# GpSimd makes the rotation table and the C powers of the second to fourth state space batch; the fine table is laid by group

## Chip, cores and metric

One Trainium2 chip, one of its cores. The metric is the device time of one execution in microseconds, lower is better; the time of a kernel is the median of its runs.

## The reference

A trunk of two layers is applied to two requests (512 and 256 tokens of width 1024) with shared weights, in float32. Layer 0 mixes tokens with two head groups side by side, a state space mixer (S5) and a gated linear attention; layer 1 with differential attention. Each is followed by cross-attention and an MLP. The change lies in the S5 mixer of layer 0, which for 32 groups of 16 channels with 64 complex states computes, in both directions:

```python
lam_bar = jnp.exp(lam * step)
b_bar = ((lam_bar - 1.0) / lam)[..., None] * b
bu = jnp.einsum('gpc,blgc->blgp', b_bar, u)
# scan over l: s[l] = lam_bar * s[l-1] + bu[l]
return jnp.einsum('gcp,blgp->blgc', c, states).real
```

and then `gelu(y_fwd + y_bwd + d * u)`. Outputs are the trunk's results for both requests.

## The kernel before

`mixer_in` projects the input of layer 0 by 17 weight tiles of 128x1024 (numbers 0 to 16; each split into a rounded high part by ScalarE and a residue by DVE in `low`, L477) and computes S5 in between. All 768 tokens lie along the free axis, cut into 96 chunks of `SC` = 8 steps. The 32 groups go in `NB` = 4 batches of `GB` = 8 groups.

In a batch everything inside a chunk is matrix products, and the recurrence runs over the 96 chunks. Its steps:
- `dve_vv`: on DVE, B times powers of lam_bar for the batch, 12 instructions of 128x512; `pe_vt` transposes them.
- `dve_cl` (L497): on DVE, C times powers, the tile `cl`, two halves of 6 instructions of 128x640, each `cl<-cc,qf`, `tmp<-cc,qf`, `cl<-cl,tmp`. From the second batch on it waits for y_done, since TensorE reads the old `cl` until then.
- `pe_lag` (L368): products of `cl` and `bbar`, 64 short matmuls; waits for the semaphore m_cl. `act_rt` copies them out, `dve_rt` (L525) adds the diagonal and signals m_rtr.
- `pe_bu` (L379): the chunk inputs; waits for m_rtr and for the load of u.
- `dve_rot` (L514): on DVE, the rotation table `rot` (cosine and sine of the chunk's angle) from `fine` (16 small steps) and `coarse` (6 large ones), four multiplications of 128x768 with broadcast operands and two additions.
- `dve_main` (L531): turns the chunk inputs by `rot`, scans over the chunks, turns back, and signals m_st (below: S). `pe_y` (L388) then forms y and signals m_yd.
- `dve_gelu`, `act_tanh`, `dve_gelu_end`, `store_y`.

Each engine runs its own list in written order, and engines meet only by semaphores; `Chain` makes an engine wait for its own last result where the next instruction reads it. TensorE's order from S of one batch to `pe_bu` of the next is: `pe_y`, `pe_vt`, a weight tile (t3), `pe_lag`, a weight tile (t4, in the first transition alone), `pe_bu`; then tiles t1 and t2 beside `dve_main`:

```python
BATCH = [(6, 7, 8, 9), (10, 11, 12, 17), (13, 14, 15, 17), (16, 17, 17, 17)]
```

17 means no tile. On SP's DMA queue `load_u` of the next batch stands behind the store of a v tile, which waits until TensorE has transposed it, after its tile t3. GpSimd has no instruction in the mixer.

Of the kernel before, what the change touches and what calls it, by code (L numbers as in the profile page):

```python
# [123 lines left out]
def build(nc, params, x_in, mem_in, wt_in, wglu_in, wgate_in, bc_in, tab_in, u_dram, y_dram, k_dram, v_dram, qk_dram, vog_dram,  # L124
          lr_dram, out):
    ctx = ExitStack()
    with ctx:
        def sb(name, shape, dt=F32, on=ctx):
            return on.enter_context(nc.sbuf_tensor(name, shape, dt))
# [36 lines left out]
        def mixer_in():  # L166
# [13 lines left out]
            S = {n: sm[:, i, :] for i, n in enumerate(names)}  # L180
            fine = sb("s5fine", [P, 2, 17, G], on=fs)
            coarse = sb("s5coarse", [P, 2, 6, G], on=fs)
# [3 lines left out]
            qr = sb("qr", [P, 2, SC, G], on=fs)  # L186
            pw = sb("pw", [P, 2, SC + 1, G], on=fs)
            bin_ = sb("bin", [P, 2, G, GC], on=fs)
            dd = sb("dd", [GC, G, GC], on=fs)
# [32 lines left out]
            sqd, acd, ssum, sroot, an, ah, ar = (sig(f"m_{n}") for n in ("sqd", "acd", "ssum", "sroot", "an", "ah", "ar"))  # L222
            dec_ready = sig("m_dec")
            ud, ul, t_v, vt_done, vt_ready, cl_ready, lag_done, rt_copied, rt_ready, m_loaded = (sig(f"m_{n}") for n in (
# [265 lines left out]

            def dve_cl(v, b):
                spare = stf if b == 0 else free_words
                tmp = spare[:, 0:4 * POS * GC].rearrange("p (g n c) -> p g n c", g=4, n=POS)
                if b > 0:
                    v.wait_ge(y_done.sem, b)
                for h in range(2):
                    hs = slice(GB * b + 4 * h, GB * b + 4 * h + 4)  # L497
                    cb = [cc[:, i, hs, :].unsqueeze(2).to_broadcast([P, 4, POS, GC]) for i in range(2)]
                    qb = [qf[:, i, :, hs].rearrange("p n g -> p g n").unsqueeze(3).to_broadcast([P, 4, POS, GC]) for i in range(2)]
                    o = [cl[:, i, 4 * h:4 * h + 4] for i in range(2)]  # L500
                    for i, op in ((0, ALU.add), (1, ALU.subtract)):
                        nc.vector.tensor_tensor(o[i], cb[0], qb[i], ALU.mult)
                        dve_chain(nc.vector.tensor_tensor(tmp, cb[1], qb[1 - i], ALU.mult))
                        last = nc.vector.tensor_tensor(o[i], o[i], tmp, op)
                        if h == 1 and i == 1:
                            last.then_inc(cl_ready.sem, 1)
                        else:
                            dve_chain(last)

            def dve_rot(v, b):  # L510
                gs = slice(GB * b, GB * b + GB)
                four = [t_.rearrange("p (g a c) -> p g a c", g=GB, c=16) for t_ in (sq3[:, 0, :], sq3[:, 1, :])]
                o = [t_[:, :, :].rearrange("p g (a c) -> p g a c", c=16) for t_ in rot]
                f = [fine[:, i, 0:16, gs].rearrange("p c g -> p g c").unsqueeze(2).to_broadcast([P, GB, 6, 16]) for i in range(2)]  # L514
                c = [coarse[:, i, :, gs].rearrange("p a g -> p g a").unsqueeze(3).to_broadcast([P, GB, 6, 16]) for i in range(2)]
                nc.vector.tensor_tensor(o[0], f[0], c[0], ALU.mult)
                if b > 0:
                    v.wait_ge(yg_ready.sem, b)
                nc.vector.tensor_tensor(four[0], f[1], c[1], ALU.mult)
                nc.vector.tensor_tensor(o[1], f[0], c[1], ALU.mult)  # L520
                dve_chain(nc.vector.tensor_tensor(four[1], f[1], c[0], ALU.mult))
                nc.vector.tensor_tensor(o[0], o[0], four[0], ALU.subtract)
                dve_chain(nc.vector.tensor_tensor(o[1], o[1], four[1], ALU.add))

            def dve_rt(v, b):  # L525
# [5 lines left out]
            def dve_main(v, b, first, second):  # L531
                low(v, first)
                v.wait_ge(bu_done.sem, b + 1)
                bur = banks(4, 1024).rearrange("p (g j) -> p g j", j=P)[:, :, 0:NCH]
                bui = banks(6, 1024).rearrange("p (g j) -> p g j", j=P)[:, :, 0:NCH]
# [55 lines left out]
            with nc.Block() as block:  # L591
# [86 lines left out]
                def _(a):  # L678
# [69 lines left out]
                    act_chain.close()  # L748

                @block.vector  # L750
                def _(v):
# [72 lines left out]
                    v.wait_ge(t_v.sem, 1)  # L824
                    dve_cl(v, 0)
                    low(v, 4)
# [4 lines left out]
                    late = quarters(sq3[:, 1:3, :])  # L831
                    for to in (fine, coarse):
                        nc.vector.memset(to[:, 0, 0, :], 1.0)
                        nc.vector.memset(to[:, 1, 0, :], 0.0)
                    cmul(fine[:, 0, 1, :], fine[:, 1, 1, :], S["p4r"], S["p4i"], S["p4r"], S["p4i"], tmp)
                    for n in (1, 2, 4, 8):
                        powers(fine, n, n, n, late)
                    nc.vector.tensor_copy(coarse[:, 0, 1, :], fine[:, 0, 16, :])
                    dve_chain(nc.vector.tensor_copy(coarse[:, 1, 1, :], fine[:, 1, 16, :]))
                    powers(coarse, 1, 1, 1, late)  # L840
# [3 lines left out]
                                                      ident[0:GC, 0:GC].unsqueeze(1).to_broadcast([GC, G, GC]), ALU.mult))  # L844
                    dve_rot(v, 0)
                    nc.vector.tensor_scalar(gains[:, 1:2], pcol("dnorm"), 1.0 - LAMBDA_INIT, None, ALU.mult)
# [6 lines left out]
                    for b in range(NB):  # L853
                        t1, t2, t3_, t4_ = BATCH[b]
                        dve_main(v, b, t1, t2)
                        if b + 1 < NB:
                            low(v, t3_)
                            dve_vv(v, b + 1)
                        if b == NB - 1:
                            for k in range(4):  # L860
                                dve_mem_apply(v, k)
                            for k in range(4):
                                dve_mem_residue(v, k)
                                dve_mem_apply(v, k + 4)
                            dve_mem_residue(v, 4)
                            dve_mem_residue(v, 5)
                        dve_gelu(v, b)
                        if b + 1 < NB:
                            dve_cl(v, b + 1)
                        dve_gelu_end(v, b)  # L870
                        if b == NB - 1:
                            dve_mem_residue(v, 6)
                            dve_mem_residue(v, 7)
                        if b + 1 < NB:
                            low(v, t4_)
                            dve_rot(v, b + 1)
                            dve_rt(v, b + 1)
# [1514 lines left out]
```

## Time and profile before

| | |
|---|---|
| median of 3 runs | 2552.81 us (2550.39 to 2553.39) |
| profiled execution | 2552.52 us, its span 2550.7 us |
| TensorE busy | 2441.4 us, 96% |
| DVE busy | 1531.6 us, 60% |
| ScalarE busy | 1149.9 us, 45% |
| GpSimd busy | 0.2 us |

The mixer with its four batches takes the first 289 us of it; the state space batches lie between 91 and 284 us. The execution's own time is 1.8 us longer than the span, which is what lies outside the trace.

### The profile page before, as it was taken

The page shows a single profiled execution, that of the slowest core. Times are in us where ns is not written, and L with a number is a line of the kernel's source. Part 1 is how long each engine was busy: PE and PEld are TensorE (multiplying, and loading weights), DVE is VectorE, ACT ScalarE, POOL GpSimd, SP SyncE. Part 2 cuts the span into 40 slices and gives each one's busy share as a digit, 9 for nine tenths or more (in the row PEclk, how much of TensorE's full clock was granted, in tenths as well). Part 3 has the DMA queues.
Part 4 walks back from the last instruction along what each step waited for, and adds up shares of the span by engine and source line. Part 5 has one row for each costly group of instructions (what it writes and reads, how often), then busy time and mean ns, then how long its engine had stood idle before and what let it go on. Part 6 is the DMA issues. An engine that isn't in the chain of part 4 may idle for free.

```text
span 2550.7 us, 35203 instructions
## 1 busy us (share of the span) xinstructions
PE 2441.4 (96%) x14102; PEld 2073.6 (81%) x14102; DVE 1531.6 (60%) x2587; ACT 1149.9 (45%) x2003; POOL 0.2 (0%) x4
## 2 busy tenths in 40 slices
PE   7997699899998999999999999999999999999999
PEld 4887576778887999899778888778788888888887
DVE  8998766767546655565565446566886545633332
ACT  4332336445433555544454344445665443433322
POOL 0000000000000000000000000000000000000000
PEclk9998899999999999999999999999999999999999
DMA  5324432255321455444224323223324322433232
GB/s 189 94 75 96 154 117 90 83 170 191 110 75 58 149 183 183 131 125 137 86 75 149 116 79 120 75 83 104 94 92 135 115 91 91 141 99 94 96 99 91
DMA packets 109667, 289.24 MB, mean 113 GB/s; under 512 B 18913, under 2 KB 41569, under 8 KB 108225
## 3 DMA queue, kind: packets, MB, share of 16 engines
q1 hardware_dynamic: 101392, 261.36, 33.1%
q10 hardware_dynamic: 8112, 25.63, 3.0%
q8 instruction: 113, 1.85, 0.3%
q14 instruction: 50, 0.40, 0.0%
HBM read 265.35 MB, written 19.50 MB: 112 GB/s over the span
## 4 chain that ended last, share of the span: by engine, by line
PE 76%; DVE 8%; ACT 3%; issue 1%; ACTq 0%; DVEq 0%
PE ps L1381 65%; PE ps L1469 2%; PE ps L1444 2%; PE ps L1487 1%; DVE wlo L1358 1%; PE ps L1511 1%; DVE ps L1662 1%; DVE ps L1661 1%; DVE yP L1663 1%; ACT yP L1530 1%; PE ps L1413 1%; PE ps L1892 1%; DVE ringP L1733 1%; PE ps L1500 0%; ACT yP L1531 0%
## 5 line engine op out<-in xcount | busy, mean ns | idle before, releaser
L1381 PE MATMUL ps<-in_hP,whi 128*128 128x512 f32 x1344 | 544.9, 405 | 6.6 <-DVE wlo L1358 2.8
L1358 DVE TENSOR_TENSOR wlo<-wraw,whi 128x1024 fp32r<-128x1024 f32 x432 | 524.7, 1218 | 35.8 <-ACT whi L1353 35.6
L1353 ACT ACTIVATE whi<-wraw 128x1024 fp32r<-128x1024 f32 x432 | 454.2, 1052 | 188.0 <-PE ps L1381 129.5
L1381 PE MATMUL ps<-in_hP,wlo 128*128 128x512 f32 x1344 | 526.8, 392 | 0.0
L1381 PE MATMUL ps<-in_lP,whi 128*128 128x512 f32 x1344 | 525.9, 391 | 0.0
L1381 PE MATMUL ps<-in_hS,whi 128*128 128x256 f32 x1088 | 320.1, 294 | 7.4 <-DVE x L1684 4.3
L1381 PEld LDWEIGHTS ps<-in_hP,whi 128*128 128x128 f32 x1344 | 254.2, 189 | 69.3 <-issue 11.3
L1381 PE MATMUL ps<-in_lS,whi 128*128 128x256 f32 x1088 | 309.5, 284 | 0.0
L1381 PE MATMUL ps<-in_hS,wlo 128*128 128x256 f32 x1088 | 309.4, 284 | 0.0
L1684 DVE TENSOR_TENSOR x<-ps,x 128x256 f32<-128x256 f32 (+1 forms) x192 | 106.9, 557 | 331.6 <-PE ps L1381 331.2
L1381 PEld LDWEIGHTS ps<-in_lP,whi 128*128 128x128 f32 x1344 | 254.3, 189 | 56.0 <-issue 5.0
L1381 PEld LDWEIGHTS ps<-in_hP,wlo 128*128 128x128 f32 x1344 | 253.8, 189 | 54.7
L1381 PEld LDWEIGHTS ps<-in_hS,whi 128*128 128x128 f32 x1088 | 210.3, 193 | 23.0 <-issue 16.7
L1381 PEld LDWEIGHTS ps<-in_lS,whi 128*128 128x128 f32 x1088 | 210.5, 193 | 2.3 <-issue 1.4
L1381 PEld LDWEIGHTS ps<-in_hS,wlo 128*128 128x128 f32 x1088 | 210.3, 193 | 0.0
L1381 PE MATMUL ps<-hid_hP,whi 128*128 128x512 f32 x512 | 202.0, 395 | 0.0
L1381 PE MATMUL ps<-hid_hP,wlo 128*128 128x512 f32 x512 | 199.4, 389 | 0.0
L1381 PE MATMUL ps<-hid_lP,whi 128*128 128x512 f32 x512 | 199.4, 389 | 0.0
L1694 DVE TENSOR_TENSOR hid_lP<-ps,hid_hP 128x512 fp32r<-128x512 f32 x64 | 44.3, 692 | 231.9 <-ACT hid_hP L1586 231.9
L1584 ACT ACTIVATE ps<-ps 128x512 f32<-128x512 f32 (+1 forms) x128 | 60.8, 475 | 244.8 <-PE ps L1381 244.8
L1381 PE MATMUL ps<-hid_hS,whi 128*128 128x256 f32 x512 | 147.8, 289 | 1.9 <-DVE x L1684 1.9
L1381 PE MATMUL ps<-hid_lS,whi 128*128 128x256 f32 x512 | 144.8, 283 | 0.0
(464 smaller groups left out, 3659.1 us busy)
## 6 DMA issues: line engine op xcount, KB each, us to landing
wraw<-wt SPq DMA_DIRECT2D x432, 512.0 KB, 3.5
wraw<-wt ACTq DMA_DIRECT2D x17, 512.0 KB, 4.2
k_scratch<-region_P SPq DMA_DIRECT2D x16, 256.0 KB, 3.1
v_scratch<-vtmp SPq DMA_DIRECT2D x32, 128.0 KB, 3.1
x<-x_in SPq DMA_DIRECT2D x4, 768.0 KB, 7.0
mix_u<-x SPq DMA_DIRECT2D x32, 64.0 KB, 3.3
mix_mem<-mem_in ACTq DMA_DIRECT2D x4, 512.0 KB, 6.4
x<-x_in ACTq DMA_DIRECT2D x1, 2048.0 KB, 12.8
```

The source lines that it names most:

```text
L1353: nc.scalar.activation(whi[:, n % NHI, :, :], wraw[:, ws(n), :, :], ACT.Copy).then_inc(wh.sem, 1)
L1358: nc.vector.tensor_tensor(wlo[:, ws(n), :, :], wraw[:, ws(n), :, :], whi[:, n % NHI, :, :].bitcast(F32), ALU.subtract).then_inc(wr.sem, 1)
L1381: last = nc.tensor.matmul(ps[:, m % 2, 0:N[prod.g]], w_[:, k, :], x_[:, k, :], start=(k == 0 and j == 0), stop=(k == KT - 1 and j == 2))
L1413: nc.tensor.matmul(ps[:, 2, 0:s.n], s.mat, ring[g][:, i % 2, :], start=True, stop=True).then_inc(z["ssum"].sem, 1)
L1444: last = nc.tensor.matmul(ps[:, 3 + q_ % 2, b * 256:(b + 1) * 256], qx[g][:, 2 * h + j, lo:lo + P], km[g][:, 2 * h + j, :], start=(j == 0) ...
L1469: last = nc.tensor.matmul(ps[:, 7, j * 256:(j + 1) * 256], vm[g][:, kt, (2 * h + j) * P:(2 * h + j + 1) * P], at[:, q_ % 2, kt * 256:(kt + ...
L1487: last = nc.tensor.matmul(ps[:, 3 + zz, 0:N[g]], dq[g][rows, h, b * P:(b + 1) * P], dk[g][rows, h, :], start=True, stop=True)
L1511: last = nc.tensor.matmul(ps[:, 6 + h % 2, b * P:(b + 1) * P], dv[g][:, j, h * P:(h + 1) * P], at[:, q_ % 2, j * P:(j + 1) * P], start=(j ...
L1530: act_chain(nc.scalar.activation(s.to[:, 0:s.n], ps[:, s.bank, 0:s.n], ACT.Ln, bias=pcol("eps"), scale=1.0 / s.width))
L1584: act_chain(nc.scalar.activation(acc_ps, acc_ps, ACT.Relu))
L1684: nc.vector.tensor_tensor(x[:, i, cols(g)], ps[:, b, 0:N[g]], x[:, i, cols(g)], ALU.add).then_inc(tf[b].sem, 1)
L1694: nc.vector.tensor_tensor(hid_l[g][:, i, :], ps[:, b, 0:N[g]], hid_h[g][:, i, :].bitcast(F32), ALU.subtract)\
```

## The change

`dve_cl` and `dve_rot` stay on DVE for the first batch alone. For batches 1 to 3 a new GpSimd list holds `pool_rot` and `pool_cl` with the same instructions. `pool_rot` waits for m_st of the batch before, since DVE reads the old table until then; it puts its intermediate products into memory of tables no longer used (`turned`, in `s5tabs`), and signals m_rot, for which `dve_main` now waits. `pool_cl` waits for m_yd and signals m_cl, as before. `fine` is laid [2, G, 17] in place of [2, 17, G], so that its innermost step in the table's multiplications is one element; its powers are written with that layout.

```diff
-            fine = sb("s5fine", [P, 2, 17, G], on=fs)
+            fine = sb("s5fine", [P, 2, G, 17], on=fs)
...
-            pw = sb("pw", [P, 2, SC + 1, G], on=fs)
-            bin_ = sb("bin", [P, 2, G, GC], on=fs)
+            tabs = sb("s5tabs", [P, 2 * (SC + 1) * G + 2 * G * GC], on=fs)
+            pw = tabs[:, 0:2 * (SC + 1) * G].rearrange("p (i n g) -> p i n g", i=2, g=G)
+            bin_ = tabs[:, 2 * (SC + 1) * G:].rearrange("p (i g c) -> p i g c", i=2, g=G)
+            turned = [tabs[:, T * i:T * i + T] for i in range(2)]
...
+            def pool_cl(g, b):
+                g.wait_ge(y_done.sem, b)
+                for h in range(2):
+                    tmp, cb, qb, o = c_operands(b, h, free_words)
+                    for i, op in ((0, ALU.add), (1, ALU.subtract)):
+                        nc.gpsimd.tensor_tensor(o[i], cb[0], qb[i], ALU.mult)
+                        pool_chain(nc.gpsimd.tensor_tensor(tmp, cb[1], qb[1 - i], ALU.mult))
+                        last = nc.gpsimd.tensor_tensor(o[i], o[i], tmp, op)
+                        if h == 1 and i == 1:
+                            last.then_inc(cl_ready.sem, 1)
+                        else:
+                            pool_chain(last)
...
-                f = [fine[:, i, 0:16, gs].rearrange("p c g -> p g c").unsqueeze(2).to_broadcast([P, GB, 6, 16]) for i in range(2)]
+                f = [fine[:, i, gs, 0:16].unsqueeze(2).to_broadcast([P, GB, 6, 16]) for i in range(2)]
...
+            def pool_rot(g, b):
+                g.wait_ge(st_ready.sem, b)
+                four, o, f, c = turn_operands(b, turned)
+                nc.gpsimd.tensor_tensor(o[0], f[0], c[0], ALU.mult)
+                nc.gpsimd.tensor_tensor(four[0], f[1], c[1], ALU.mult)
+                nc.gpsimd.tensor_tensor(o[1], f[0], c[1], ALU.mult)
+                pool_chain(nc.gpsimd.tensor_tensor(four[1], f[1], c[0], ALU.mult))
+                nc.gpsimd.tensor_tensor(o[0], o[0], four[0], ALU.subtract)
+                nc.gpsimd.tensor_tensor(o[1], o[1], four[1], ALU.add).then_inc(rot_ready.sem, 1)
...
                 v.wait_ge(bu_done.sem, b + 1)
+                if b > 0:
+                    v.wait_ge(rot_ready.sem, b)
...
+                @block.gpsimd
+                def _(g):
+                    pool_chain.start(g)
+                    for b in range(1, NB):
+                        pool_rot(g, b)
+                        pool_cl(g, b)
+                    pool_chain.close()
...
                         dve_gelu(v, b)
-                        if b + 1 < NB:
-                            dve_cl(v, b + 1)
                         dve_gelu_end(v, b)
...
                             low(v, t4_)
-                            dve_rot(v, b + 1)
                             dve_rt(v, b + 1)
```

On DVE of the kernel before, from the last `cl` instruction of the second batch to the start of the second `dve_main` (`sq`, `vv` and `x` hold intermediate values, `rot_re` and `rot_im` the table):

```order
L504 TENSOR_TENSOR cl<-cl,x 128x640 [waits dchain]
L565 SCALAR_TENSOR_TENSOR sq<-sq 128x768 [waits m_ye2]
L477 TENSOR_TENSOR wlo<-wraw,whi 128x1024 [waits m_wh]
L516 TENSOR_TENSOR rot_re<-s5fine,s5coarse 128x768
L519 TENSOR_TENSOR sq<-s5fine,s5coarse 128x768 [waits m_ygr]
L520 TENSOR_TENSOR rot_im<-s5fine,s5coarse 128x768
L521 TENSOR_TENSOR sq<-s5fine,s5coarse 128x768
L522 TENSOR_TENSOR rot_re<-rot_re,sq 128x768 [waits dchain]
L523 TENSOR_TENSOR rot_im<-rot_im,sq 128x768
L527 TENSOR_TENSOR x<-x,ps 16x8x16 [waits m_rtc,dchain]
L528 TENSOR_TENSOR x<-x,dd 16x8x16 [waits dchain]
```

The same place on DVE in the changed kernel, from the last instruction of `dve_vv`:

```order
L267 TENSOR_TENSOR vv<-mix_u 128x512
L589 SCALAR_TENSOR_TENSOR sq<-sq 128x768 [waits m_yc]
L595 SCALAR_TENSOR_TENSOR sq<-sq 128x768 [waits m_ye2]
L480 TENSOR_TENSOR wlo<-wraw,whi 128x1024 [waits m_wh]
L555 TENSOR_TENSOR x<-x,ps 16x8x16 [waits m_rtc]
L556 TENSOR_TENSOR x<-x,dd 16x8x16 [waits dchain]
L480 TENSOR_TENSOR wlo<-wraw,whi 128x1024 [waits m_wh]
L259 TENSOR_TENSOR sq<-ps,rot_re 128x768 [waits m_rot,m_bu]
```

The 12 `cl` rows between L559 and L565 and the six rows L516 to L523 are gone, and the first instruction of `dve_main` has a second semaphore to wait for, m_rot.

GpSimd's list in the changed kernel begins, behind its memsets, with the table of the second batch and goes on to `cl`:

```order
L546 TENSOR_TENSOR rot_re<-s5fine,s5coarse 128x768 [waits m_st]
L547 TENSOR_TENSOR s5tabs<-s5fine,s5coarse 128x768
L548 TENSOR_TENSOR rot_im<-s5fine,s5coarse 128x768
L549 TENSOR_TENSOR s5tabs<-s5fine,s5coarse 128x768
L550 TENSOR_TENSOR rot_re<-rot_re,s5tabs 128x768 [waits m_pool]
L551 TENSOR_TENSOR rot_im<-rot_im,s5tabs 128x768
L518 TENSOR_TENSOR cl<-cc,qf 128x640 [waits m_yd]
L519 TENSOR_TENSOR x<-cc,qf 128x640
L520 TENSOR_TENSOR cl<-cl,x 128x640 [waits m_pool]
```

The table, which stood behind `cl` on DVE, stands ahead of it here. The three `cl` rows come four times, then the next batch's table; 54 rows in all. TensorE's list is unchanged: its lag product (L371) waits for m_vtr and m_cl.

## Rows read from the trace of the kernel before

**Rows 1.** The page: busy time, share of the span and instructions of each engine.
```profile
PE 2441.4 (96%) x14102; PEld 2073.6 (81%) x14102; DVE 1531.6 (60%) x2587; ACT 1149.9 (45%) x2003; POOL 0.2 (0%) x4
```

**Rows 2.** Busy time by stretch (us); the last columns are granted clock, DMA share, GB/s.
```profile
91.30:94.20 2.90, 2.90 (x67) 2.69 (x65) 0.34 (x1) 1.44 (x2) 0.00 (x0) 1.00 0.59 141
...
243.70:248.80 5.10, 0.00 (x0) 0.00 (x0) 5.00 (x7) 1.79 (x2) 0.00 (x0) 0.72 0.46 122
248.80:253.70 4.90, 4.76 (x65) 4.68 (x66) 1.14 (x2) 0.00 (x0) 0.00 (x0) 0.59 0.53 64
```

**Rows 3.** Timeline of DVE: start us, duration us, line, operation; ends of `dve_main`, then the next work.
```profile
112.61 0.07 DVE L554 MEMSET x<- 64x8 f32 x1
112.70 1.23 DVE L477 TENSOR_TENSOR wlo<-wraw,whi 128x1024 fp32r<-128x1024 f32 x1
...
120.84 0.68 DVE L264 TENSOR_TENSOR vv<-mix_u 128x512 f32<-128x512 f32 x1
...
166.19 0.07 DVE L554 MEMSET x<- 64x8 f32 x1
...
220.25 0.07 DVE L554 MEMSET x<- 64x8 f32 x1
```

**Rows 4.** Timeline of TensorE: last y product, transposes, lag products (L368), input products (L379).
```profile
117.78 0.61 PE L390 MATMUL ps<-x,cl 128*128 128x96 f32 x4
121.58 1.97 PE L357 MATMUL ps<-par,vv 128*128 128x128 f32 x16 [3.20 <-DVE vv L264]
...
132.14 1.06 PE L368 MATMUL ps<-cl,bbar 64*16 64x128 f32 x16 [0.25 <-DVE cl L504]
...
188.91 3.68 PE L368 MATMUL ps<-cl,bbar 64*16 64x128 f32 x64
...
196.66 0.42 PE L379 MATMUL ps<-x,mix_u 128*64 128x96 f32 x1 [4.07 <-DMA x<-u_scratch]
...
239.94 3.68 PE L368 MATMUL ps<-cl,bbar 64*16 64x128 f32 x64 [0.38 <-DVE cl L504]
...
248.94 0.39 PE L379 MATMUL ps<-x,mix_u 128*64 128x96 f32 x1 [5.31 <-DVE x L528]
```

**Rows 5.** Timeline of ScalarE and DVE behind the second and third lag product.
```profile
194.87 0.28 DVE L528 TENSOR_TENSOR x<-x,dd 16x128 f32<-16x128 f32 x1
...
244.49 1.00 ACT L460 ACTIVATE x<-ps 16x1024 f32<-16x1024 f32 x1
...
248.51 0.28 DVE L528 TENSOR_TENSOR x<-x,dd 16x128 f32<-16x128 f32 x1
```

**Rows 6.** Timeline: one of each kind of instruction, GpSimd's memset and DVE's.
```profile
0.23 0.10 POOL L2381 MEMSET const-float32-0.0<- 128x1 f32 x1 [0.23 <-issue]
...
100.89 3.40 DVE L541 TENSOR_TENSOR_SCAN x<-x 128x768 f32<-128x768 f32 x2
...
121.44 0.95 DVE L559 SCALAR_TENSOR_TENSOR sq<-sq 128x768 f32<-128x768 f32 x1
122.31 0.82 DVE L502 TENSOR_TENSOR cl<-cc,qf 128x640 f32<-128x640 f32 x1
...
240.67 1.48 DVE L516 TENSOR_TENSOR rot_re<-s5fine,s5coarse 128x768 f32<-128x768 f32 x1
...
246.34 0.96 DVE L522 TENSOR_TENSOR rot_re<-rot_re,sq 128x768 f32<-128x768 f32 x1
```

**Rows 7.** Timeline of DVE and TensorE ahead of the first batch.
```profile
71.77 0.19 DVE L256 TENSOR_TENSOR sq<-s5fine 128x32 f32<-128x32 f32 x1
...
76.97 0.42 DVE L264 TENSOR_TENSOR s5fine<-sq 128x256 f32<-128x256 f32 x1
...
90.23 0.28 DVE L528 TENSOR_TENSOR x<-x,dd 16x128 f32<-16x128 f32 x1
...
91.39 0.30 PE L379 MATMUL ps<-x,mix_u 128*64 128x96 f32 x1
...
94.30 0.96 DVE L256 TENSOR_TENSOR sq<-ps,rot_re 128x768 f32<-128x768 f32 x1 [2.65 <-PE ps L380]
```

More of the change, by code:

```diff
@@ L222, in mixer_in @@
             sqd, acd, ssum, sroot, an, ah, ar = (sig(f"m_{n}") for n in ("sqd", "acd", "ssum", "sroot", "an", "ah", "ar"))
-            dec_ready = sig("m_dec")
+            dec_ready, rot_ready = sig("m_dec"), sig("m_rot")
+            pool_chain = Chain(sig("m_pool"))
             ud, ul, t_v, vt_done, vt_ready, cl_ready, lag_done, rt_copied, rt_ready, m_loaded = (sig(f"m_{n}") for n in (
@@ L489, in dve_vv, with c_operands, dve_cl @@
                     cmul(o[0], o[1], bb[0], bb[1], qq[0], qq[1], ta, done=t_v if h else None)
-            def dve_cl(v, b):
-                spare = stf if b == 0 else free_words
+            def c_operands(b, h, spare):
                 tmp = spare[:, 0:4 * POS * GC].rearrange("p (g n c) -> p g n c", g=4, n=POS)
-                if b > 0:
-                    v.wait_ge(y_done.sem, b)
+                hs = slice(GB * b + 4 * h, GB * b + 4 * h + 4)
+                cb = [cc[:, i, hs, :].unsqueeze(2).to_broadcast([P, 4, POS, GC]) for i in range(2)]
+                qb = [qf[:, i, :, hs].rearrange("p n g -> p g n").unsqueeze(3).to_broadcast([P, 4, POS, GC]) for i in range(2)]
+                return tmp, cb, qb, [cl[:, i, 4 * h:4 * h + 4] for i in range(2)]
+            def dve_cl(v):
                 for h in range(2):
[L497 to L500, printed above, removed]
+                    tmp, cb, qb, o = c_operands(0, h, stf)
                     for i, op in ((0, ALU.add), (1, ALU.subtract)):
@@ L508, in dve_cl, with turn_operands, dve_rot @@
                             dve_chain(last)
-            def dve_rot(v, b):
+            def pool_cl(g, b):
[10 more added lines that the diff above has]
+                            pool_chain(last)
+            def turn_operands(b, spare):
                 gs = slice(GB * b, GB * b + GB)
-                four = [t_.rearrange("p (g a c) -> p g a c", g=GB, c=16) for t_ in (sq3[:, 0, :], sq3[:, 1, :])]
+                four = [t_.rearrange("p (g a c) -> p g a c", g=GB, c=16) for t_ in spare]
                 o = [t_[:, :, :].rearrange("p g (a c) -> p g a c", c=16) for t_ in rot]
-                f = [fine[:, i, 0:16, gs].rearrange("p c g -> p g c").unsqueeze(2).to_broadcast([P, GB, 6, 16]) for i in range(2)]
+                f = [fine[:, i, gs, 0:16].unsqueeze(2).to_broadcast([P, GB, 6, 16]) for i in range(2)]
                 c = [coarse[:, i, :, gs].rearrange("p a g -> p g a").unsqueeze(3).to_broadcast([P, GB, 6, 16]) for i in range(2)]
+                return four, o, f, c
+            def dve_rot(v):
+                four, o, f, c = turn_operands(0, (sq3[:, 0, :], sq3[:, 1, :]))
                 nc.vector.tensor_tensor(o[0], f[0], c[0], ALU.mult)
-                if b > 0:
-                    v.wait_ge(yg_ready.sem, b)
                 nc.vector.tensor_tensor(four[0], f[1], c[1], ALU.mult)
@@ L824, in _ @@
                     v.wait_ge(t_v.sem, 1)
-                    dve_cl(v, 0)
+                    dve_cl(v)
                     low(v, 4)
@@ L831, in _ @@
                     late = quarters(sq3[:, 1:3, :])
[L832 to L835, printed above, removed]
-                    for n in (1, 2, 4, 8):
-                        powers(fine, n, n, n, late)
-                    nc.vector.tensor_copy(coarse[:, 0, 1, :], fine[:, 0, 16, :])
-                    dve_chain(nc.vector.tensor_copy(coarse[:, 1, 1, :], fine[:, 1, 16, :]))
+                    for to in (fine[:, :, :, 0], coarse[:, :, 0, :]):
+                        nc.vector.memset(to[:, 0, :], 1.0)
+                        nc.vector.memset(to[:, 1, :], 0.0)
+                    cmul(fine[:, 0, :, 1], fine[:, 1, :, 1], S["p4r"], S["p4i"], S["p4r"], S["p4i"], tmp)
+                    grouped = [q.rearrange("p n g -> p (n g)").rearrange("p (g n) -> p g n", n=8) for q in late]
+                    for n in (1, 2, 4, 8):
+                        by = [fine[:, i, :, n:n + 1].to_broadcast([P, G, n]) for i in range(2)]
+                        cmul(fine[:, 0, :, n + 1:2 * n + 1], fine[:, 1, :, n + 1:2 * n + 1], fine[:, 0, :, 1:n + 1], fine[:, 1, :, 1:n + 1],
+                             by[0], by[1], [q[:, :, 0:n] for q in grouped])
+                    nc.vector.tensor_copy(coarse[:, 0, 1, :], fine[:, 0, :, 16])
+                    dve_chain(nc.vector.tensor_copy(coarse[:, 1, 1, :], fine[:, 1, :, 16]))
                     powers(coarse, 1, 1, 1, late)
@@ L844, in _ @@
                                                       ident[0:GC, 0:GC].unsqueeze(1).to_broadcast([GC, G, GC]), ALU.mult))
-                    dve_rot(v, 0)
+                    dve_rot(v)
                     nc.vector.tensor_scalar(gains[:, 1:2], pcol("dnorm"), 1.0 - LAMBDA_INIT, None, ALU.mult)
```

## Prediction

> **What bounds the kernel now.** The page says that TensorE is busy 96% of the span and DVE 60%, and GpSimd 0.2 us in all [rows 1]. That average hides the place of the change, so I read the busy time by stretch next, over the state space batches (112 to 279 us). There TensorE is the fuller engine while it has projection tiles, and empty in short stretches, 5.1 us at 243.7 for one [rows 2]. Outside these batches the change touches nothing, and what it does inside shifts the rest rigidly.
>
> The timeline gives the chain of one batch. I call S the moment at which `dve_main` signals its states (end of its last memset): 112.68, 166.26 and 220.32 us for the first three batches [rows 3]. From S, TensorE forms y (end 118.39), waits for `dve_vv` of the next batch (end S + 8.8), transposes it at 121.58, runs one weight tile, and comes to the lag product `pe_lag`, which needs `cl`. It starts at 132.14, 188.91 and 239.94, which is S + 19.46, S + 22.65 and S + 19.62 [rows 4]. In the first and third it waited 0.25 and 0.38 us for DVE's last `cl` instruction; in the second it did not wait. The 3.20 us before the transposes are a wait for `dve_vv`. Then two ACTIVATEs and two small DVE additions give `rt_ready`, which `pe_bu` needs. In the second transition `rt_ready` (195.15) is 1.5 us earlier than `pe_bu` (196.66), which waits for the load of u; in the third `pe_bu` waits 5.31 us for DVE, because the rotation table stands ahead of the additions [rows 4, 5].
>
> So DVE's 12 `cl` instructions and 6 rotation instructions are nearly all under TensorE's tiles. **The most that their removal can bring** is 0.3 us, 0 us and, in the third, 0.3 us and the wait behind the rotation table: copies end 245.49, additions 0.6 us, so 246.1 in place of 248.79, which is 2.7 us [rows 5]. Together 3.3 us, if GpSimd is always in time.
>
> **What the change costs.** It puts 6 + 12 = 18 instructions of two SBUF operands on GpSimd, in order, three times. No row shows such an instruction there; its memsets of one element take 0.10 us, DVE's of eight 0.07 us, so the fixed part shown is small [rows 3, 6]. Lower bound for the rest: DVE's own 0.95 us for 128x768 and 0.82 us for 128x640. 
>
> The table waits for S. `cl` waits for y_done (S + 5.7 by the first batch), which has passed when the table is done at S + 10.2. So with no disturbance `cl` is ready at S + 27.2, and the lag product, which was at S + 19.5, is late. Behind it on TensorE stand the second weight tile of the batch and `pe_bu`, and for `pe_bu` waits the whole next `dve_main`; nothing covers this. The table itself is needed only by `dve_main`, long after, so its new wait costs nothing, but it stands in front of `cl` in GpSimd's queue.
>
> **Both engines read SBUF.** In that stretch DVE runs one weight residue and the 12 instructions of `dve_vv` (8.8 us), `dve_gelu` and `dve_gelu_end` (0.95 us each) and in the first batch one more residue (1.2 us): 10.7 us, or 11.9 in the first, all of two SBUF operands [rows 3, 6]. What sharing costs no row shows; the ends are nothing and the full sum. I take the full sum. The row that bears on it: the same multiplication of 128x768 took 1.48 us where `s5fine` was read with a stride, and 0.95 us from plain operands, so reading, not arithmetic, already sets an instruction's time, and I see no spare reading for a second engine [rows 6]. The Trainium skill, "SBUF — State Buffer", Who interferes with whom, speaks against this change: a DVE instruction with two SBUF inputs and a GpSimd instruction that reads SBUF lock each other out for a whole instruction. By it the two loads add; without it they overlap.
>
> With the loads added `cl` is ready at S + 27.2 + 11.9 = S + 39.1 in the first transition and S + 37.9 in the others. Late: 39.1 - 19.5 = 19.6; 37.9 - 22.65 = 15.3; 37.9 - 19.6 = 18.3 us. At `pe_bu` 19.6 us remain of the first. The second had 1.5 us of slack: 13.8. The third gets back the 2.7 us of the table: 15.6. Sum 49.0 us.
>
> TensorE then stands idle about 10 us or more before each lag product. In a shorter idle stretch the granted clock already falls: 0.72 at 243.7 and 0.59 behind it, so mostly at the 1.2 GHz level, where `pe_bu` has 4.76 us of busy time; the first `pe_bu`, behind tiles without a gap, has 2.90 us at 1.00 [rows 2]. The lag product is as many matmuls as short, so I charge it 2.0 us in each transition: 6 us. Total +55 us.
>
> **Nothing, or nearly.** `fine` is laid with the group outside. DVE still makes the first table: four multiplications of about 1.5 us [rows 6] become at best 0.95, 2.2 us less; the powers of `fine` (24 instructions from 71.77 to 77.39, 5.6 us) may cost up to 60% more by the same strided row, 3.4 us. Both lie before `dve_rt` ends at 90.51, 0.9 us before TensorE's first `pe_bu` at 91.39, and DVE then waits 2.65 us for it: between 0 and +0.1 us, I take 0 [rows 7]. The new name `s5tabs` only shares memory of tables that are dead by then. DMA issues are the same in number and order; `store_y` may come earlier, since `dve_gelu_end` is no longer behind `cl`, and no one waits for it.
>
> The sum is made against the profiled execution, 2552.5 us (span 2550.7), which is 0.3 us under the median 2552.8: 2552.5 + 55 = 2607.5 us.
>
> **Rivals.**
> 1. Loads added, as above: 2607. With GpSimd's instructions 25% shorter or longer, 6.8 us in each transition: 2587 to 2628. Chance 0.47.
> 2. The engines take strict turns, one instruction each. Then `dve_vv` is late too: its last of 13 instructions ends behind 13 of GpSimd (6 x 1.70 + 7 x 1.42 = 20.1 us), at S + 28.9, TensorE's transposes are 20.1 us late, and the second transition loses its slack, since the load of u stands behind the v tile in SP's queue. 20.0 + 20.1 + 17.2 + 6 = 63: 2616. For it: DVE's vv has pauses at its chained waits only, against it as well, since four instructions at a time start before the last has ended. Chance 0.08.
> 3. No disturbance between the engines. `cl` at S + 27.2: late 7.7, 4.6 - 1.5 = 3.1 and 7.6 - 2.7 = 4.9, sum 15.7, with 6 us for the clock 22: 2574; with the 25%, 2554 to 2594. Nothing in the trace speaks against it but the row on reading. Chance 0.28.
> 4. Not slower: GpSimd streams at DVE's rate and undisturbed. Table 5.7 us, `cl` 12 x 0.82 = 9.9: ready at S + 15.7, before the tile is out of the way; all 3.3 us come: 2549. It decides when table and `cl` together stay under 19.4 us, that is 0.71 of my scan rate (1.21 us for 128x768). Chance 0.12, of which most gives less than the 5.1 us that 0.2% are.
> 5. Worse than all these (instructions twice the scan rate): above 2628. Chance 0.05.
>
> **Numbers.** A measurement here tells about 0.2% (5 us) from no change. Faster by more 0.04, since even the best case ends at 0.13%; within 0.2% 0.09, case 4 and the low edge of case 3; slower 0.87. The range takes the likeliest case, the turns, and case 3 without its lowest part: 2562 to 2628. The likeliest case alone is 2587 to 2628.
>
> **What would show it.** GpSimd rows of about 1.7 and 1.4 us, 54 in all. The wait of the lag product (L371) on GpSimd's `cl` (L520) of some 7 us without disturbance and 15 with it, three times. `dve_vv` instructions spread from 0.69 us each: if they stay there beside a running GpSimd, case 3 holds. The period from S to S, 53.6 us now, at about 75 in the first transition. The wait of the third `pe_bu` for DVE should fall from 5.3 us to about 2.5. I would be wrong if GpSimd is fast (case 4), or if its reads and DVE's overlap.

## The result, and the profile after

| | before | changed |
|---|---|---|
| median | 2553.10 us (4 runs, 2550.39 to 2554.87) | 2601.38 us (4 runs, 2601.31 to 2602.38) |
| ratio | | 1.019, 95% interval 1.0178 to 1.0202 |
| profiled span | 2550.7 us | 2599.5 us |

The change costs 48.3 us. The forecast was 2607 us (+55 us on the profiled execution) in a range of 2562 to 2628. Two of the twelve executions of layout_only below were slow ones (2639.72 and 4829.88 us); its ratio leaves them out, and without them its median is 2552.75 us. The page's busy times, against [rows 1], with POOL as GpSimd:

```profile
PE 2445.8 (94%) x14102; PEld 2076.6 (80%) x14102; DVE 1531.4 (59%) x2533; ACT 1150.8 (44%) x2003; POOL 98.9 (4%) x58
```

DVE's busy time is unchanged although it has 54 instructions less, and GpSimd has 98.9 us. S, the end of `dve_main`'s last memset, stands at 113.11 us in the first batch and then here (timeline of DVE; start, duration):

```profile
183.52 0.07 DVE L584 MEMSET x<- 64x8 f32 x1
...
251.19 0.07 DVE L584 MEMSET x<- 64x8 f32 x1
...
316.41 0.07 DVE L584 MEMSET x<- 64x8 f32 x1
```

So the four S are 113.11, 183.59, 251.26 and 316.48, against 112.68, 166.26, 220.32 before [rows 3] and 270.92 for the fourth. (The first S moves by itself: it lies between 111.5 and 113.1 us in the ten kernels whose code up to there is the same. So periods from S to S are compared below, or this is kept in mind.) The periods are 70.5, 67.7 and 65.2 us in place of 53.6, 54.1 and 50.6: +16.9, +13.6 and +14.6, together 45.1 us. Where they come from stands in the timelines of the two engines side by side. GpSimd in the first transition:

```profile
113.19 2.61 POOL L546 TENSOR_TENSOR rot_re<-s5fine,s5coarse 128x768 f32<-128x768 f32 x1 [112.75 <-DVE x L584]
115.76 2.02 POOL L547 TENSOR_TENSOR s5tabs<-s5fine,s5coarse 128x768 f32<-128x768 f32 x1
...
126.10 1.77 POOL L518 TENSOR_TENSOR cl<-cc,qf 128x640 f32<-128x640 f32 x1
127.84 1.77 POOL L519 TENSOR_TENSOR x<-cc,qf 128x640 f32<-128x640 f32 x1
...
142.42 1.35 POOL L518 TENSOR_TENSOR cl<-cc,qf 128x640 f32<-128x640 f32 x1
...
145.15 1.57 POOL L520 TENSOR_TENSOR cl<-cl,x 128x640 f32<-128x640 f32 x1
```

DVE in the same time:

```profile
113.04 0.07 DVE L584 MEMSET x<- 64x8 f32 x1
113.14 1.23 DVE L480 TENSOR_TENSOR wlo<-wraw,whi 128x1024 fp32r<-128x1024 f32 x1
114.28 2.06 DVE L259 TENSOR_TENSOR mix_u<-bbar,qr 128x512 f32<-128x512 f32 x1
116.27 2.05 DVE L260 TENSOR_TENSOR mix_u<-bbar,qr 128x512 f32<-128x512 f32 x1
...
128.34 1.81 DVE L260 TENSOR_TENSOR mix_u<-bbar,qr 128x512 f32<-128x512 f32 x1
...
135.48 2.01 DVE L267 TENSOR_TENSOR vv<-mix_u 128x512 f32<-128x512 f32 x1
```

DVE's `dve_vv` instructions of 128x512, 0.68 us each in [rows 3], take 1.7 to 2.3 us, and they start in step with GpSimd's: 114.28, 116.27 on one, 115.76 with its next at 117.74 on the other. One instruction of each makes a pair of 1.98 us. How the two share is seen at the start: DVE's weight residue (L480) began at 113.14, 0.05 us ahead of GpSimd's first instruction, and took 1.23 us as before [rows 3], while GpSimd's took 2.61 us, about its own time (1.57 us alone, below) and what was left of the residue. So the one that begins first is not slowed, and the other waits for nearly the whole of it; they do not share bit by bit. The last `dve_vv` instruction ends at 137.49, S + 24.4, instead of S + 8.8. After one more gelu instruction of DVE GpSimd is alone, and `cl<-cc,qf` falls from 1.77 to 1.35 us. TensorE (timeline; in brackets idle time before and who ended it):

```profile
137.55 3.65 PE L360 MATMUL ps<-par,vv 128*128 128x128 f32 x16 [18.73 <-DVE vv L267]
...
149.46 3.68 PE L371 MATMUL ps<-cl,bbar 64*16 64x128 f32 x64
...
208.02 3.67 PE L360 MATMUL ps<-par,vv 128*128 128x128 f32 x16 [18.72 <-DVE vv L267]
...
228.56 0.30 PE L382 MATMUL ps<-x,mix_u 128*64 128x96 f32 x1 [3.69 <-DMA x<-u_scratch]
...
294.78 0.39 PE L382 MATMUL ps<-x,mix_u 128*64 128x96 f32 x1 [2.63 <-DVE x L556]
```

The transposes (L360) wait 18.7 us for `dve_vv`, in all three transitions, where it was 3.20 us in the first [rows 4]; each time they start at S + 24.4 and not S + 8.9, 15.5 us late. The lag product (L371) waits for nobody: GpSimd had finished `cl` at 146.72, 2.7 us before TensorE came to it. The granted clock by stretch (last columns: clock, DMA share, GB/s):

```profile
113.10:140.20 27.10, 8.22 (x61) 8.09 (x62) 26.27 (x15) 2.15 (x3) 26.62 (x14) 0.64 0.15 47
140.20:149.40 9.20, 9.20 (x53) 8.17 (x51) 2.10 (x2) 7.09 (x14) 6.28 (x5) 0.95 0.07 13
```

It falls in the 27 us to 140.2, in which TensorE has 8.2 us of work, and the transposes run at the low clock (3.65 us instead of 1.97); a weight tile follows them, so that the lag product has the full clock again, 3.68 us as before.

### The profile page after: what moved, and what is told of

The parts are those of the page before. It is cut to its first block, busy times and chain, and to the rows that moved or that the text cites. A ratio compares the mean times of both kernels' runs of the same rounds, so it can differ in the third digit from the quotient of the medians.

```text
span 2599.5 us, 35205 instructions
## 1 busy us (share of the span) xinstructions
PE 2445.8 (94%) x14102; PEld 2076.6 (80%) x14102; DVE 1531.4 (59%) x2533; ACT 1150.8 (44%) x2003; POOL 98.9 (4%) x58
## 4 chain that ended last, share of the span: by engine, by line
PE 74%; DVE 8%; ACT 3%; issue 1%; ACTq 0%; DVEq 0%
PE ps L1419 64%; PE ps L1507 2%; PE ps L1482 2%; PE ps L1525 1%; DVE wlo L1396 1%; PE ps L1549 1%; DVE ps L1700 1%; DVE ps L1699 1%; DVE yP L1701 1%; ACT yP L1568 1%; PE ps L1451 1%; PE ps L1930 1%; PE ps L1538 0%; PE ps L1495 0%; ACT yP L1569 0%
## 5 line engine op out<-in xcount | busy, mean ns | idle before, releaser
L1419 PEld LDWEIGHTS ps<-in_hP,wlo 128*128 128x128 f32 x1344 | 254.0, 189 | 54.9
```

The source lines that it names most:

```text
L1419: last = nc.tensor.matmul(ps[:, m % 2, 0:N[prod.g]], w_[:, k, :], x_[:, k, :], start=(k == 0 and j == 0), stop=(k == KT - 1 and j == 2))
```

## Experiments

Each was timed against the kernel before on the same chip. Where "leaves out" is said, the time is read without regard to the output's values. In all of them S is read as above.

**The layout alone (layout_only).** All 18 instructions a batch are back on DVE.

```diff
-                    for b in range(1, NB):
-                        pool_rot(g, b)
-                        pool_cl(g, b)
...
+                        if b + 1 < NB:
+                            dve_cl(v, b + 1)
...
+                            dve_rot(v, b + 1)
                             dve_rt(v, b + 1)
```

> The changed kernel with all tables and C powers back on DVE, at their old places; only the layout of the fine table is new (and the memory of s5tabs). If the layout is what I costed it at, the four table multiplications fall from about 1.5 to about 0.95 us each and only the third transition gains, about 2.2 us, where TensorE's input product waited 5.3 us for DVE: about 2550.5 us. If the layout or the grouping of its powers cost something on the path, it would be above 2553 us. Against the changed kernel it must show that the whole loss is GpSimd's part, about 50 us less.

Measured 2553.18 us, ratio 1.0 (0.9991 to 1.0009). DVE's timeline shows the table's multiplications:

```profile
80.35 0.96 DVE L538 TENSOR_TENSOR rot_re<-s5fine,s5coarse 128x768 f32<-128x768 f32 x1
81.22 0.95 DVE L541 TENSOR_TENSOR sq<-s5fine,s5coarse 128x768 f32<-128x768 f32 x1
```

They cost 0.95 us and not 1.48 [rows 6]. The fourth S stands at 267.56, 3.4 us earlier than before; 1.1 of these lie ahead of the first S, and 2.3 in the three periods, as expected in sum. Not one by one: they are 54.9, 51.9 and 49.2 us against 53.6, 54.1 and 50.6. In the third the input products wait 3.24 us for DVE and no longer 5.31, the 2.1 us of the layout, but take 0.7 us longer; in the first the transposes take 3.14 us for 1.97, in the second u is there 1.5 us sooner. The total is not shorter: from the fourth S to the end the span has 2284.5 us, before 2279.8. Most of the difference arises in one stretch of unchanged code. Busy time and clock there, this kernel and then the kernel before in the same stretch counted from the fourth S:

```profile
736.00:886.00 150.00, 140.92 (x841) 126.31 (x840) 90.81 (x152) 66.48 (x129) 0.00 (x0) 0.95 0.31 96
```

```profile
739.40:889.40 150.00, 140.92 (x876) 127.74 (x874) 93.92 (x157) 68.14 (x131) 0.00 (x0) 0.99 0.33 102
```

TensorE is busy 140.92 us in both, but the granted clock is 0.95 against 0.99 and 35 matmuls fewer are done. All eleven profiles fall into two groups. Six kernels have 0.95 there and 2282.8 to 2284.6 us from the fourth S to the end (the changed one, layout_only, cpowers_only, behind_bpowers, table_behind_rt, residue_behind); five have 0.99 and 2279.5 to 2280.1 us (before, table_only, write_only, one_operand, beside_main). That accounts for most of the 3.2 us by which the changed kernel's span grew beyond its fourth S (48.8 against 45.6), and it means that a few us gained or lost in the mixer can be covered by it. It need not be the kernel's own: three executions of layout_only took 2549.3 to 2549.7 us, seven 2551.9 to 2554.0. What decides the clock there was not tried.

**One part at a time (table_only, cpowers_only).** In the first GpSimd's list has `pool_rot` alone, in the second `pool_cl` alone; the other is on DVE at its old place.

```diff
                     for b in range(1, NB):
                         pool_rot(g, b)
-                        pool_cl(g, b)
```

> GpSimd makes the rotation table alone; the C powers are back on DVE. Theory of turns (a GpSimd and a DVE instruction of two SBUF operands take turns and each pair takes about 2 us): six pairs of about 2 us while DVE has the residue and the first six instructions of the B powers, so the transposes are about 8.5 us late in each transition, the third gets 2.7 us back: +23 us, about 2576 us. Theory that only GpSimd's own time and the new wait cost (no disturbance): the table is needed only much later, so nothing is late: about 2549 us.

Measured 2577.05 us, ratio 1.0099 (1.0086 to 1.0112); its transposes:

```profile
129.00 3.68 PE L360 MATMUL ps<-par,vv 128*128 128x128 f32 x16 [11.79 <-DVE vv L267]
```

A table that nobody needs for another 30 us costs 24.6 us. Under the theory of turns 23 were expected; without disturbance it would have been free. The first six `dve_vv` instructions are stretched by GpSimd's six, the last six are back at 0.69 us, and the transposes wait 11.79, 11.77 and 10.15 us.

> GpSimd makes the C powers alone; the table is on DVE. Theory of turns: GpSimd starts only at y_done, 5.7 us behind S, and slows the last five or so of the B powers' instructions: transposes some 6 us late in each transition, third transition 2.2 us back through the layout: +16 us, about 2569 us, and the lag product again does not wait for GpSimd. Theory of no disturbance: the C powers of 12 x 1.35 us are ready at S + 22, so the lag products are 2.5, 0 and 2.5 us late: about 2555 us.

Measured 2574.91 us, ratio 1.0086 (1.0073 to 1.0099). More than I expected, and the lag product did wait for GpSimd (timeline of TensorE, first and third transition):

```profile
139.69 3.68 PE L371 MATMUL ps<-cl,bbar 64*16 64x128 f32 x64 [1.70 <-POOL cl L520]
...
260.30 6.46 PE L371 MATMUL ps<-cl,bbar 64*16 64x128 f32 x64 [6.28 <-POOL cl L520]
```

Started at y_done, GpSimd first slows the rest of `dve_vv` (transposes 4.6 us late) and is itself slowed by it, then at its end by a weight residue and the first multiplication of the table on DVE (2.36 and 2.28 us there), so `cl` is ready only at S + 27.2. In the third transition five of the table's instructions on DVE are stretched to 2.1 to 2.3 us beside it, and the lag product, after its wait, takes 6.46 us. I had counted the collision in one direction. The two parts add up to 24.6 + 22.4 = 47.0 us, close to the whole 48.3.

**No collision with the B powers (behind_bpowers).**

```diff
             def pool_rot(g, b):
                 g.wait_ge(st_ready.sem, b)
+                g.wait_ge(t_v.sem, b + 1)
```

> The changed kernel with GpSimd's list of a batch held until DVE has finished the B powers of that batch (a wait on their semaphore). Theory of turns: the B powers are back at 0.69 us each and end at S + 8.8; GpSimd's instructions run at about 1.57 us for 128x768 and 1.3 us for 128x640 and the C powers are ready at about S + 35, so now the lag product waits for GpSimd, 16 us late, 11 and 13 in the other transitions: +40 to 46 us, 2593 to 2599 us, little less than the changed kernel though nothing collides. If collisions were not what lengthens the B powers, they would stay near 2 us each here as well.

Measured 2606.67 us, ratio 1.0208 (1.0193 to 1.0223), against 1.019 for the changed kernel: no better, rather 5 us worse. GpSimd with SBUF to itself, table and C powers:

```profile
124.17 1.57 POOL L548 TENSOR_TENSOR s5tabs<-s5fine,s5coarse 128x768 f32<-128x768 f32 x1
125.70 1.57 POOL L549 TENSOR_TENSOR rot_im<-s5fine,s5coarse 128x768 f32<-128x768 f32 x1
...
128.90 1.84 POOL L551 TENSOR_TENSOR rot_re<-rot_re,s5tabs 128x768 f32<-128x768 f32 x1
...
147.13 1.33 POOL L518 TENSOR_TENSOR cl<-cc,qf 128x640 f32<-128x640 f32 x1
148.42 1.33 POOL L519 TENSOR_TENSOR x<-cc,qf 128x640 f32<-128x640 f32 x1
149.82 1.53 POOL L520 TENSOR_TENSOR cl<-cl,x 128x640 f32<-128x640 f32 x1
```

TensorE in the same transition:

```profile
121.97 3.67 PE L360 MATMUL ps<-par,vv 128*128 128x128 f32 x16 [3.20 <-DVE vv L267]
...
151.41 5.19 PE L371 MATMUL ps<-cl,bbar 64*16 64x128 f32 x64 [16.62 <-POOL cl L520]
```

The transposes are back at a wait of 3.20 us, so it is the overlap that lengthens `dve_vv`. Now the lag product waits 16.62 us for GpSimd, 16.08 and 18.16 in the others: the wait that I had forecast appears when the collision is taken away. It starts at S + 38.4. GpSimd alone starts a multiplication of 128x768 every 1.53 us and one of 128x640 every 1.30 us; its additions are slower, 1.84 and 1.53 us, and a wait for its own result costs about 0.1 us. Put together from undisturbed instructions (9.9 us for the table, 4.3 for each three of `cl`) its 18 instructions need 27.1 us; here they take 29.3 us from 122.07, since DVE's gelu instructions and a weight residue fall into them. I expected S + 35, from the multiplications' times alone. The granted clock also told: the lag product took 5.19 us, and 6.21 and 5.83 us in the others.

**What of GpSimd collides (write_only, one_operand).** All 18 instructions become memsets of the same outputs in the one, copies of the first operand in the other; the products and sums of batches 1 to 3 are left out.

```diff
-                        nc.gpsimd.tensor_tensor(o[i], cb[0], qb[i], ALU.mult)
+                        nc.gpsimd.memset(o[i], 0.5)
```

> The changed kernel with each of GpSimd's 18 instructions a batch replaced by a memset of the same output; this leaves out the values of the table and the C powers of batches 1 to 3. If only GpSimd's reads stand in DVE's way, the B powers stay at 0.69 us each beside running memsets and the time is that of a GpSimd for free: about 2549 us. If GpSimd's writes block DVE too, they are spread as in the changed kernel (1.7 to 2.3 us).

Measured 2549.12 us, ratio 0.9987 (0.9977 to 0.9997). GpSimd's first memset and its first on `cl`:

```profile
112.12 0.74 POOL L546 MEMSET rot_re<- 128x768 f32 x1 [111.68 <-DVE x L584]
...
117.84 0.63 POOL L518 MEMSET cl<- 128x640 f32 x1 [1.48 <-PE ps L393]
```

DVE beside them:

```profile
113.24 0.68 DVE L259 TENSOR_TENSOR mix_u<-bbar,qr 128x512 f32<-128x512 f32 x1
113.84 0.68 DVE L260 TENSOR_TENSOR mix_u<-bbar,qr 128x512 f32<-128x512 f32 x1
```

TensorE's transposes:

```profile
120.97 2.82 PE L360 MATMUL ps<-par,vv 128*128 128x128 f32 x16 [3.20 <-DVE vv L267]
```

DVE does not notice 18 writes of the same size. And this is the gain of a GpSimd that costs nothing: 3.2 us by the medians, beside the 3.3 us of the forecast's upper bound. The periods are 54.9, 51.8 and 47.3 us. The first two are those of layout_only within 0.1; the third is 3.4 us shorter than before, where the forecast has 3.0. There the input products start only 1.5 us sooner, since the transposes take 3.62 us for 1.97, but then take 2.9 us for 4.7. So two effects of the clock, of 1.7 and 1.8 us, cancel in it.

> The changed kernel with each of GpSimd's 18 instructions replaced by a copy of its first operand into the same output; this leaves out the products and sums of batches 1 to 3. If any read by GpSimd excludes a DVE instruction of two SBUF operands, the B powers still take turns with it, each DVE instruction shows its own 0.6 us and the copy's time; copies should be shorter than 1.3 to 1.6 us, so the transitions lengthen by less than in the changed kernel: some 2565 to 2590 us. If it takes two operands to collide, the B powers stay at 0.69 us.

Measured 2568.43 us, ratio 1.0064 (1.0046 to 1.0083). GpSimd's copies, beside DVE and alone:

```profile
113.88 1.30 POOL L547 COPY s5tabs<-s5fine 128x768 f32<-128x768 f32 x1
...
130.89 0.72 POOL L519 COPY x<-cc 128x640 f32<-128x640 f32 x1
```

DVE's second `dve_vv` instruction:

```profile
114.41 1.32 DVE L260 TENSOR_TENSOR mix_u<-bbar,qr 128x512 f32<-128x512 f32 x1
```

One operand read by GpSimd is enough: a copy of 128x768 beside a DVE instruction of 128x512 makes pairs of 1.25 us (from 113.88 to the next start at 115.13), and DVE's instruction is as long as the pair, 1.32 us.

**What of DVE collides (beside_main).** On the layout_only kernel, idle multiplications beside `dve_main`, whose first four read one operand from PSUM (the input products) and one from SBUF.

```diff
+                    for b in range(1, NB):
+                        g.wait_ge(bu_done.sem, b + 1)
+                        for _i in range(12):
+                            pool_chain(nc.gpsimd.tensor_tensor(turned[_i % 2][:, 0:640], qpool, qpool2, ALU.mult))
```

> The layout_only kernel plus 12 idle GpSimd multiplications of 128x640 with two SBUF operands, started when TensorE's input products are done, in the second to fourth batch: they run beside dve_main, which begins with four multiplications of one PSUM and one SBUF operand. Theory of turns for two SBUF operands alone: those four stay at 0.95 us beside a running GpSimd, and the additions, the residue and the scan behind them, which read SBUF twice, lengthen. If any DVE instruction collides, the first four lengthen as well. The three batches together 15 to 30 us longer than layout_only.

A single execution was timed: 2590.66 us, 37.5 us above layout_only, more than expected. The timeline of DVE:

```profile
150.32 0.96 DVE L261 TENSOR_TENSOR sq<-ps,rot_re 128x768 f32<-128x768 f32 x1 [8.34 <-PE ps L385]
151.20 0.95 DVE L262 TENSOR_TENSOR vv<-ps,rot_im 128x768 f32<-128x768 f32 x1
...
152.93 0.95 DVE L264 TENSOR_TENSOR sq<-ps,rot_re 128x768 f32<-128x768 f32 x1
153.91 2.17 DVE L265 TENSOR_TENSOR x<-sq,vv 128x768 f32<-128x768 f32 x1
156.00 2.32 DVE L267 TENSOR_TENSOR x<-sq,vv 128x768 f32<-128x768 f32 x1
...
160.74 6.10 DVE L575 TENSOR_TENSOR_SCAN x<-x 128x768 f32<-128x768 f32 x2
...
177.87 0.95 DVE L584 TENSOR_TENSOR x<-sq,vv 64x760 f32<-64x760 f32 x1
```

All GpSimd multiplications together (min, median, max in ns; start times):

```profile
L790 POOL TENSOR_TENSOR s5tabs<-cc,qf x36: 1562/2128/2908, 150.4 to 303.0; 128x640 f32<-128x640 f32 x36
```

The four instructions with an operand in PSUM take 0.95 us each while GpSimd runs; the next, the same count from two SBUF operands, 2.17 us. The two scans take 6.10 us instead of 3.40 [rows 6]. When GpSimd has ended, L584 is back at 0.95 us. Undisturbed too is GpSimd beside the four: its first instruction there takes 1.59 us, while the median of all 36 is 2.13. The two engines read different tiles here, so it is no matter of one tile read by both.

**Without GpSimd (table_behind_rt, residue_behind).** Two orders on DVE that the profiles point to, both with the new layout. In the first `dve_rot` stands behind `dve_rt`, in the second the weight residue `low` of tile t3 behind the B powers:

```diff
                         if b + 1 < NB:
-                            low(v, t3_)
                             dve_vv(v, b + 1)
+                            low(v, t3_)
```

> No GpSimd: the layout_only kernel with the rotation table of the next batch moved behind dve_rt on DVE. rt_ready then never waits for the table, which DVE makes while TensorE forms the input products (4.7 us; the table takes 4.3 us). The third transition gains up to 0.6 us more than layout_only, the others nothing, unless the table ends later than the input products and dve_main starts late: 2549 to 2551 us.

Measured 2555.26 us, ratio 1.0009 (1.0 to 1.0018): no gain. Its `dve_main` starts late: the fourth S is at 271.0, 3.4 us behind layout_only, 2.6 of them from the third transition. There TensorE's input products end at 251.9 and DVE, with the table (to 252.6) and a weight residue still to make, begins `dve_main` at 253.77.

> No GpSimd: the layout_only kernel with DVE's weight residue of tile t3 moved behind the B powers of the next batch (12 instructions, 7.6 us). TensorE waited 3.2 us for the B powers in the first transition and the residue of 1.2 us stood ahead of them; tile t3 needs it only after 2 us of transposes. So each of three transitions should gain 1.1 us, 3.4 us together against layout_only, about 2550 us, if the B powers bound the transitions as the changed kernel suggests; no gain if the wait is for something else. The granted clock of the later stages moves the total by some 4 us whatever the mixer does, so the test is where the fourth batch's S stands (267.56 us in layout_only), expected at 264.2.

Measured 2548.35 us, ratio 0.9981 (0.9972 to 0.999), faster than both kernels. The wait for the B powers falls from 3.20 us [rows 4] to:

```profile
119.64 1.97 PE L360 MATMUL ps<-par,vv 128*128 128x128 f32 x16 [2.06 <-DVE vv L267]
```

and the fourth batch's last memset stands at

```profile
262.56 0.07 DVE L586 MEMSET x<- 64x8 f32 x1
```

that is S = 262.63, 4.9 us earlier than in layout_only, and 5.2 us counted from the first S. In each of the three transitions the transposes start at S + 7.8 and no longer S + 8.9, 3 x 1.14 = 3.4 us, the amount expected. The rest is mostly the clock: in the second transition the transposes take 1.97 us for the 3.42 of layout_only. In the first they are shorter too (1.97 for 3.14), but there the lag product now waits 1.39 us for `cl`. The best version found is a reordering on DVE, worth 4.6 us.

## Why the prediction was right, and where it was not

- **The bound.** That the DVE instructions taken away lay under TensorE's tiles, and that their removal brings at most 3.3 us, is shown by write_only, 3.2 us in all and 3.4 us in the third transition, where 3.0 were forecast; that it came so near is luck in part, as two effects of the clock cancel there. The prediction rests on this and on the next point, and both hold.
- **Both engines' loads add when DVE and GpSimd read SBUF.** Shown three ways: `dve_vv` at 0.68 us without GpSimd's reads and 2.0 with them, write_only, beside_main. The Trainium skill, "SBUF — State Buffer", Who interferes with whom, has this distinction (two SBUF inputs on DVE against a GpSimd instruction that reads SBUF, not one that only writes), and the runs agree with each of these, the four DVE instructions with one operand in PSUM included (0.95 us beside GpSimd). Why they lock each other out, no run here shows. The reasoning from the strided row on reading was an argument, no measurement; the layout changed that cost to 0.95 us without making room for GpSimd.
- **What failed: the order in which the engines take turns.** The prediction took as likeliest that `dve_vv` runs through and the lag product waits for `cl` until S + 39.1. The runs show strict turns, the second rival, which had a chance of 0.08: the transposes wait for `dve_vv` (18.73 us) and the lag product for nothing. The prediction let DVE's time delay GpSimd and charged nothing for GpSimd's time to DVE, though a lock works both ways. I had thought that DVE's overlapping starts would keep GpSimd out between chained waits. In the changed kernel they do not; GpSimd gets every second place. The forecast of 7 or 15 us of wait at L371 was wrong (0 us); the period of 75 us from the first S to the second was 70.5, and the wait of the third `pe_bu`, forecast at 2.5 us, was 2.63. The remark that `dve_vv` instructions spread from 0.69 us if the engines collide was the one that told.
- **The size of a turn.** I had 1.70 us for each of GpSimd's 128x768 and 1.42 for 128x640, 27.2 us for the 18. Undisturbed they need 27.1 us, so the sum was right, though neither size was: the multiplications, with broadcast operands, are shorter (1.57 and 1.33 us, 1.53 and 1.30 from start to start), the additions, with plain ones, longer (1.84 and 1.53). That DVE's scan gave about the right sum was luck. Too large was what the second rival charged `dve_vv`: 13 instructions, 20.1 us. DVE's residue began first and lost nothing, so it was 12, and they cost 15.5 us, since a pair takes 1.98 us where the two starts alone make 1.53 + 0.60 = 2.13. So `dve_vv` ended at S + 24.4, not at S + 28.9. By the ratio of the Trainium skill's "GPSIMD Engine Reference", Performance versus the Vector engine (1.96 for an addition), an estimate, 128x768 would take 1.86 us and 128x640 1.61. The additions agree within 5% (1.84 and 1.53), the multiplications are shorter.
- **The clock.** I charged 2.0 us to the lag product in each transition, 6 us. It ran at full clock; the transposes paid instead, since the idle time lay ahead of them: 1.7 us in the first and third transition (3.65 and 3.67 against 1.97), and nothing in the second, where they had taken 3.67 us before the change too. So 3.4 of the 6 us were there. Where the lag product does stand behind the idle time, in behind_bpowers, it pays 1.5 to 2.5 us.
- **The sum.** Transitions +16.9, +13.6, +14.6 against 21.6, 15.8, 17.6 forecast. Each has the 15.5 us of the transposes, the first and third 1.7 us of the clock besides. In the second the input products, still behind the load of u, are 14.6 us late and take 1.0 us less than before; in the third they get back 2.7 us of waiting for DVE. To these come 0.4 us before the first S and 3.2 us behind the last, the latter mostly a clock stretch in unchanged code, which no term of the forecast covers. The total was good by luck in part. The wrong wait and the right one have nearly the same length, as both are made of the same loads: in the first transition `cl` was ready at S + 33.6, and the lag product, held by the late transposes and the tile behind them, began at S + 36.4.
- **The table's wait and the layout.** `dve_main` never waited for m_rot. The layout gave 2.1 us per table, as costed; its powers take 0.2 us more (5.8 against 5.6), with `dve_rt` of the first batch ready 3.1 us ahead of `pe_bu`, so nothing of it shows at TensorE.

## What to carry to other kernels

Before work goes to GpSimd, look at what DVE does in that stretch: where both read SBUF and DVE needs two SBUF operands, they take turns, and that can cost far more than it gives, even for a result that nobody waits for (24.6 us for the table). What stretches then is DVE's own critical work, so the wait turns up at another semaphore than the one of the moved tile. GpSimd ran free beside DVE instructions with one operand in PSUM, and where it only wrote; and an engine at 60% may be relieved better by putting its instruction without hurry behind the one that is waited for.

## What the runs showed of the hardware

- GpSimd alone, two SBUF operands of float32: multiplications with broadcast operands 1.53 us for 128x768 and 1.30 us for 128x640 from start to start (2.0 ns per element of a partition), DVE 0.87 and 0.74. Additions of plain operands 1.84 and 1.53 us (2.4 ns), where DVE takes 0.95 and 0.82. A multiplication of plain operands of 128x640 took 1.59 us (beside_main), so it seems to be the operands' form and not the operation; no run tried it by itself.
- Beside DVE: pairs of 1.98 us (128x768 with 128x512), a little under the sum of both alone, one by one, for as long as both have work. GpSimd's own instruction is as long as the pair too (2.02 us). The one that has begun is not slowed (DVE's residue, 1.23 us).
- A copy on GpSimd (one SBUF operand) collides in the same way; a memset (0.74 us for 128x768) does not, nor does a DVE multiplication with one operand in PSUM. DVE's scan of two SBUF operands does: 6.10 us for two in place of 3.40.
- TensorE's granted clock: 0.64 over 27.1 us in which it had 8.2 us of work, and 0.95 in the 9.2 us behind. The same unchanged stretch of 150 us, 140.9 of them busy, had 0.95 in six kernels and 0.99 in five, worth 3 to 5 us.
